# Moving memory rows, late tables and conditioning weights back, and crossing two groups by halves, in a two-block transformer kernel

## The reference, cut to what matters

```python
mod = silu(c) @ ada_w[layer] + ada_b[layer]          # 6 x 1024
sh1, sc1, g1, sh2, sc2, g2 = split(mod, 6)
h = rmsnorm(x, norm_g[layer, 0]) * (1 + sc1) + sh1
z, xbc, dt_raw, qkv = split(h @ ab_w_in, ...)        # product "in0"
y = concat([ssd_branch(z, conv5(xbc), dt_raw), neighbourhood_attention(qkv)])
x = x + g1 * rmsnorm(y @ ab_w_out)                   # product "out0"
h = rmsnorm(x, norm_g[layer, 2]) * (1 + sc2) + sh2   # needed by product "up0"
```

## Time and profile before

| | |
|---|---|
| median of three runs | 1597.03 us (1594.93 to 1597.8) |
| profiled execution: its own time, its span | 1598.08 us, 1596.3 us |
| mean granted clock of TensorE | 0.974 of full |
| busy: PE, DVE, ACT, POOL | 93%, 72%, 50%, 5% of the span |
| chain that ended last | PE 46%, DVE 21%, PE's weight loads 15%, issue 8%, ACT 7%, DMA 2% |
| chain from 0 to 120 us, largest lines | DMA of the stream 27.2%, DVE L2182 16.3%, DVE L1310 14.7%, DVE L1171 6.6% |

### The profile page before, as it was taken

How to read it: one execution, slowest core, us unless ns; L and a number is a source line. 1 busy time by engine, 2 the same in 40 slices (tenths; PEclk the granted TensorE clock), 3 DMA queues, 4 the chain that set the end, 5 groups by cost and what they waited for, 6 DMA issues and landing times.

```text
span 1596.3 us, 22352 instructions
## 1 busy us (share of the span) xinstructions
PE 1489.3 (93%) x8907; PEld 1276.0 (80%) x8910; DVE 1142.4 (72%) x1824; ACT 791.3 (50%) x1079; POOL 83.7 (5%) x82
## 2 busy tenths in 40 slices
PE   4779998999999999999999999889999899999998
PEld 3778875789988888877899888756786578799987
DVE  6797775599866857666786567999985675466653
ACT  4646654454533536454555435556554634354442
POOL 0000000000000000000000002940020000000000
PEclk7889999999999999999999999999999899999999
DMA  9864623369778553335566555333334243245551
GB/s 387 348 232 188 237 89 121 148 238 359 286 280 332 193 180 138 132 132 211 196 229 236 174 211 193 133 106 107 131 136 163 92 149 122 90 160 184 185 191 63
DMA packets 42518, 298.57 MB, mean 187 GB/s; under 512 B 4656, under 2 KB 4912, under 8 KB 7472
## 3 DMA queue, kind: packets, MB, share of 16 engines
q1 hardware_dynamic: 39984, 283.52, 47.9%
q0 software_dynamic: 1568, 8.39, 1.4%
q10 hardware_dynamic: 864, 5.24, 0.9%
HBM read 292.94 MB, written 4.19 MB: 186 GB/s over the span
## 4 chain that ended last, share of the span: by engine, by line
PE 46%; DVE 21%; PEld 15%; issue 8%; ACT 7%; DMA 2%; PEldq 1%; SPq 0%; ACTq 0%; DVEq 0%
PE ps L1034 19%; PE ps L1042 15%; PEld ps L1034 8%; PEld ps L1042 6%; DVE ring_at_lo L1310 6%; ACT w_hi L1299 3%; PE ps L1075 2%; DMA ring_at<-stream 2%; DVE ring_at L1171 2%; PE ps L2616 1%; DVE arena_at L2182 1%; DVE arena_at L3183 1%; PE ps L3527 1%; DVE arena_at L3192 1%; PE ps L3086 1%
## 5 line engine op out<-in xcount | busy, mean ns | idle before, releaser
L1310 DVE TENSOR_TENSOR ring_at_lo<-ring_at,w_hi 128x2048 fp32r<-128x2048 f32 (+1 forms) x218 | 496.3, 2279 | 179.4 <-ACT w_hi L1299 179.0
L1299 ACT ACTIVATE w_hi<-ring_at 128x2048 fp32r<-128x2048 f32 (+1 forms) x218 | 412.3, 1898 | 191.8 <-PE ps L1034 122.9
L1034 PE MATMUL ps<-w_hi,arena_at_lo 128*128 128x512 f32 x1104 | 305.1, 398 | 1.6 <-DVEq L4476 0.8
L1042 PE MATMUL ps<-h_hi,w_hi 128*128 128x256 f32 x1440 | 243.2, 292 | 14.8 <-DVE ring_at_lo L1310 7.8
L1034 PEld LDWEIGHTS ps<-w_hi,arena_at_lo 128*128 128x128 f32 x1104 | 204.6, 188 | 49.3 <-issue 2.7
L1042 PE MATMUL ps<-h_hi,ring_at_lo 128*128 128x256 f32 x1440 | 233.2, 284 | 0.0
L1042 PE MATMUL ps<-hT_at_lo,w_hi 128*128 128x256 f32 x1440 | 232.2, 284 | 0.0
L1042 PEld LDWEIGHTS ps<-h_hi,w_hi 128*128 128x128 f32 x1440 | 202.7, 193 | 23.0 <-issue 16.6
L1042 PEld LDWEIGHTS ps<-hT_at_lo,w_hi 128*128 128x128 f32 x1440 | 200.6, 192 | 0.0
L1042 PEld LDWEIGHTS ps<-h_hi,ring_at_lo 128*128 128x128 f32 x1440 | 199.1, 192 | 0.0
L1034 PE MATMUL ps<-ring_at_lo,arena_at_lo 128*128 128x512 f32 x552 | 172.1, 393 | 0.0
(11 more groups left out here) (464 smaller groups left out, 1662.9 us busy)
## 6 DMA issues: line engine op xcount, KB each, us to landing
ring_at<-stream SPq DMA_DIRECT2D x266, 1024.0 KB, 4.9
arena_at_lo<-kept_hi POOLq DMA_DIRECT2D x4, 1024.0 KB, 7.2
arena_at<-bias ACTq DMA_DIRECT2D x4, 768.0 KB, 8.0
kept<-arena_at POOLq DMA_DIRECT2D x4, 512.0 KB, 4.2
arena_at<-kept ACTq DMA_DIRECT2D x2, 1024.0 KB, 5.9
x_res<-x SPq DMA_DIRECT2D x1, 1024.0 KB, 10.5
arena_at<-mem POOLq DMA_DIRECT2D x1, 1024.0 KB, 12.7
kept_hi<-arena_at_lo POOLq DMA_DIRECT2D x1, 1024.0 KB, 10.5
```

The source lines that it names most:

```text
L1034: mm = pe.matmul(k.ps[:, bank + t, :], x_tile(f, slice(t * P, (t + 1) * P)), w, start=first and n == 0, stop=last and n == 2)
L1042: mm = pe.matmul(k.ps[:, bank + q // 2, (q % 2) * TOK:(q % 2 + 1) * TOK], w[:, q * P:(q + 1) * P], x, start=first and n == 0 and q % 2 == ...
L1299: act.activation(k.w_hi[:, s % HI, 0:n, :], k.ring[:, c % RING, 0:n, :], ACT.Identity).then_inc(k.hi_done, 1)
L1310: dve.tensor_tensor(k.w_lo[:, c % RING, 0:n, :], k.ring[:, c % RING, 0:n, :], k.w_hi[:, s % HI, 0:n, :].bitcast(F32), ALU.subtract).then_i ...
```

## The change

1. The first four own chunks of in0 are (0,0), (1,0), narrow, (0,1), then (1,1). Groups 2 and 3 stand behind the first and the second. The opening makes the high and low part of (1,0) behind half 0 of `h`, the low part in the midst of the dots of group 2. The norm's last transposes go to another PSUM bank.
2. Groups 4, 5, 6 stand behind own chunks 12, 16, 20 of in0 instead of 2, 5, 8; groups 7, 8, 9 behind chunks 3, 5, 7 of out0 instead of 11, 14, 17 of in0. Two waits of PE for guests are dropped.
3. The load of the memory rows waits until four own chunks are used, MemRates and MemTurn move from main steps 6 to 14 to 17 to 25, BiasLoad from 16 to 28, the late tables from behind stream chunk 10 to 13, and Inputs from step 6 to 10. SsdSteps is paced from 11 instead of 8, Ssd from 16 instead of 15.

```diff
-GUESTS = {"in0": [-1, -1, 0, 0, 2, 5, 8, 11, 14, 17], "up0": ...
+GUESTS = {"in0": [-1, -1, 0, 1, 12, 16, 20], "out0": [3, 5, 7], "up0": ...
+ORDER = {"in0": [(0, 0), (1, 0), (0, 1), (1, 1)] + [(g, j) for g in range(2, 11) for j in range(2)], ...
-        own.insert(1, ("narrow", NARROW[name], 0, None))
+        own.insert(2 if name == "in0" else 1, ("narrow", NARROW[name], 0, None))
...
     def gpsimd(self, pool, st):                     # MemTurn
         pool.wait_ge(*self.norm.m["bank_turned"].at(4))
+        pool.wait_ge(k.chunk_used, self.after)      # mem_turn.after = 4
         pool.dma_start(self.rows, k.mem_dram).then_inc(k.mem_in, 16)
...
-        return (4, 5, 6, 2)[f // 2]                 # FirstNorm.bank
+        return 4 + f // 2
...
-        split_hi(k, act, self.first_own + 2)        # FirstProduct.scalar, ahead of high(1)
+        split_hi(k, act, self.first_own + 3)
...
-        self.opening_dots(dve, 2)                   # FirstProduct.vector
+        self.opening_dots(dve, 2, (0, 1))
+        split_lo(k, dve, self.first_own + 2)
+        self.opening_dots(dve, 2, (2, 3))
         self.opening_dots(dve, 3)
         self.take_opening(dve, st, 2)
         self.take_opening(dve, st, 3)
-        split_lo(k, dve, self.first_own + 2)
+        split_lo(k, dve, self.first_own + 3)
         self.norm.low(dve, 1)
...
-        pe.wait_ge(k.guest_took, self.guests)       # SsdNorm and Mlstm
...
-    steps_due = paced([(0, 7, 8, 36)])
-    ssd_due = paced([(0, 7, 15, 22), (7, 13, 22, 29), ...
+    steps_due = paced([(0, 7, 11, 36)])
+    ssd_due = paced([(0, 7, 16, 22), (7, 13, 22, 29), ...
-        Woven(k, in0, (Threaded(Inputs(k)), paced([(0, 1, 6, 7)])),
-              (Threaded(mem_rates), paced([(0, 2, 6, 10)])), (Threaded(mem_turn), paced([(0, 4, 6, 14)])),
-              (Threaded(tables), paced([(0, 1, 16, 17)])),
+        Woven(k, in0, (Threaded(Inputs(k)), paced([(0, 1, 10, 11)])),
+              (Threaded(mem_rates), paced([(0, 2, 17, 19)])), (Threaded(mem_turn), paced([(0, 4, 17, 25)])),
+              (Threaded(tables), paced([(0, 1, 28, 29)])),
...
-                if c == 10:                         # SP: the late tables
+                if c == 13:
```

More of the change, by code:

```diff
@@ L98 @@
 MEM_AT = {"up0": 0, "in1": 1, "up1": 2, "in2": 3}
-GUESTS = {"in0": [-1, -1, 0, 0, 2, 5, 8, 11, 14, 17], "up0": [1, 3, 5, 7, 9, 11], "down0": [1, 4, 7, 10, 13],
+GUESTS = {"in0": [-1, -1, 0, 1, 12, 16, 20], "out0": [3, 5, 7],
+          "up0": [1, 3, 5, 7, 9, 11], "down0": [1, 4, 7, 10, 13],
           "out1": [3], "up1": [3, 9]}
@@ L124 @@
 HALVES = [(0, 0), (1, 0), (0, 1), (1, 1)]
-ORDER = {"xo": HALVES, "mix_out": HALVES, "xq": HALVES,
+ORDER = {"in0": [(0, 0), (1, 0), (0, 1), (1, 1)] + [(g, j) for g in range(2, 11) for j in range(2)], "xo": HALVES, "mix_out": HALVES, "xq": HALVES,
          "gate_up": HALVES + [(g, j) for g in range(2, FF2T // 2) for j in range(2)]}
@@ L1232, in follow @@
         self.norm, self.cond_in = norm, cond_in
-        self.opening = self.guests_after.pop(-1) + self.guests_after.pop(0)
+        self.opening = self.guests_after.pop(-1) + self.guests_after.pop(0) + self.guests_after.pop(1)
     def tensor(self, pe):
@@ L1249, in scalar, with opening_dots @@
         self.norm.high(act, st, 0)
-        split_hi(k, act, self.first_own + 2)
+        split_hi(k, act, self.first_own + 3)
         self.norm.high(act, st, 1)
         yield from super().scalar(act, st)
-    def opening_dots(self, dve, n):
-        for q in range(4):
+    def opening_dots(self, dve, n, qs=range(4)):
+        for q in qs:
             self.guest_dots(dve, n, self.opening[n][1], q)
@@ L2223, in __init__ @@
         super().__init__(k)
-        self.first, self.guests, self.z_in = in0.first_group, k.guests, z_in
+        self.first, self.z_in = in0.first_group, z_in
         self.xc, self.zs, self.zs_r, self.xc_r, self.rows = xc, zs, zs_r, xc_r, rows
@@ L2541, with __init__ @@
 class Mlstm(Stage):
-    def __init__(self, k, qT, kT, v, o, sel, gate, h, e, sc, small, junk, hi, lo, first, guests, o_in):
+    def __init__(self, k, qT, kT, v, o, sel, gate, h, e, sc, small, junk, hi, lo, first, o_in):
         super().__init__(k)
@@ L2547, in __init__ @@
         self.h, self.e, self.sc, self.small, self.junk = h, e, sc, small, junk
-        self.hi, self.lo, self.first, self.guests, self.o_in = hi, lo, first, guests, o_in
+        self.hi, self.lo, self.first, self.o_in = hi, lo, first, o_in
         self.steps = [("cell", i) for i in range(5)] + [("norm", 0), ("cell", 5), ("turn", 0), ("cell", 6), ("turn", 1),
@@ L2601, in out @@
             if i == 0:
-                pe.wait_ge(k.guest_took, self.guests)
                 pe.wait_ge(*self.gate.m["gates_in"].at(2))
@@ L2824, in layer1_stages @@
     gate.follow(in1)
-    cell = Mlstm(k, qT, kT, v, o, sel, gate, h, e, sc, sm, junk, hi, lo, first, k.guests, o_in)
+    cell = Mlstm(k, qT, kT, v, o, sel, gate, h, e, sc, sm, junk, hi, lo, first, o_in)
     cell.after = mem
@@ L4391, in all_stages @@
     tables = BiasLoad(k, table, bias, mem_turn, mem_rates)
+    mem_turn.after = 4
     in0 = in0_stage(k, xp, xc, zs, qT, kT, v, z_in, Conditions(k, mods), first_norm, mem_turn.stored)
@@ L4398, in all_stages @@
     src = Joined(Operand(None, norm.zs_r, norm.xc_r, norm.made), KD, Operand(None, na_hi, na_lo, na.made))
-    out0 = PostProduct(k, "out0", src, y, junk, small)
+    out0 = PostProduct(k, "out0", src, y, junk, small, Conditions(k, mods))
     out0.at_row = at_c
@@ L4403, in all_stages @@
     out0.follow(gain)
-    steps_due = paced([(0, 7, 8, 36)])
-    ssd_due = paced([(0, 7, 15, 22), (7, 13, 22, 29), (13, 19, 29, 36), (19, 21, 38, 40), (21, 54, 40, 76)])
+    steps_due = paced([(0, 7, 11, 36)])
+    ssd_due = paced([(0, 7, 16, 22), (7, 13, 22, 29), (13, 19, 29, 36), (19, 21, 38, 40), (21, 54, 40, 76)])
     norm_due, na_in, na_out = paced([(0, 4, 76, 84)]), paced([(0, 6, 81, 92)]), paced([(6, 19, 0, 24)], True)
```

## The result

The changed kernel takes 1598.55 us (median of 20 runs), the kernel before 1595.97 in runs on the same chip: a ratio of 1.0018, with a 95% interval of 1.0011 to 1.0026. By the ratio it is 2.9 us slower (the medians are 2.6 apart). That is less than the 3.2 us that I count as no difference, but the interval over 20 runs leaves out 1, so the sign is sure, and it is not the sign of my forecast (1594.7). The profiled execution has a span of 1600.4 us, 4.1 more than the one before; its own time, 1602.28, lies 3.7 above the median, so its losses are on the large side.

What follows compares the result with a forecast made beforehand. Arrivals were taken to bound the opening of in0 and DVE what follows; start -5.5, later in0 +1.5 and out0 +1.7 sum to -2.3 us, so a median of 1594.7 us, range 1589.5 to 1600.5.

Steps and rivals of the forecast that it cites:

- The opening: Start of in0: (1,0) fills PE's 5.8 us gap before the narrow chunk; (0,1) starts at 48.8 instead of 46.10.
- PE waits for [the late tables] inside the narrow chunk, which costs nothing, as (0,1) waits until 48.8 anyway: Narrow chunk of in0: tables end about 47.4, and PE's wait for them costs nothing.
- The memory rows: In (1,1) of in0: issued at 56.4, landing after 7.5 us (bounds 5.4 and 12.7); PE stands 4 to 5 us.
- my list: DVE's low splits in in0 of (2,1), (3,0) and two further, forecast at 73.7, 83.8, 95.8, 102.3.
- The mark: Second crossing of `x` to rows in in0: at 113.4 instead of 118.96; the start gives 5.5 us.
- The SSD norm: Later in in0: group 6's four dots land where DVE's norm chain is the path; costs 1.5 us, bounds 0 and 4.7.
- Rival B: Dots between out0's heads stop the attention: 5 us over forecast with five on the path, all twelve 1607; chance 0.12.
- A: Start of in0: memory rows there at 59.4 and Ln finds its table, giving 11.7 us in all, 1588.5; chance 0.25.
- C: Start of in0: memory rows as slow as now, 12.7 us; the start gives 0.3, time 1599.9; chance 0.13.
- out0's term: out0: twelve dots go in, nine fit into DVE's waits, last chunks come just in time; costs 1.7 us, bounds 0.5 and 5.
- I am wrong if ... out0 grows by more than 3: Sign against the forecast: out0's length, forecast up 1.7 us, growing by more than 3.

Runs made afterwards that it cites:

- no_cross: Changed kernel with the old order of own chunks (0,0), narrow, (0,1), (1,0) and the old opening; 1602.12 us, ratio 1.0042 to the kernel before.
- rows3: Changed kernel with the memory rows loaded once three own chunks are used instead of four; 1593.65 us, ratio 0.9989 to the kernel before.
- steps: Changed kernel with the second Ln of SsdSteps placed ahead of the first Silu; 1595.58 us, ratio 1.0006 to the kernel before.
- g_late: Changed kernel with groups 4 to 8 behind in0's chunks 10, 12, 14, 16, 18 and group 9 behind out0's chunk 1; 1591.8 us, ratio 0.9975.
- inp12: Changed kernel with the wait for the late tables one main step later; 1600.65 us, ratio 1.0034 to the kernel before.
- best1: Changed kernel with the edits of rows3, inp12 and steps, and groups 7 to 9 behind out0's chunks 1, 3, 5; 1587.52 us, ratio 0.9945.
- best2: Changed kernel with the edits of rows3, inp12 and steps, and the guest groups placed as in g_late; 1582.43 us, ratio 0.9918.
- short9: Changed kernel with group 9's dots over 16 columns instead of 1024, leaving out most of its sums; 1597.81 us, ratio 1.0014.

## Why the prediction was right and wrong

- **The opening: right, but for a gap.** (1,0) runs behind the first chunk, after 1.2 us of wait for its low part, where I had no gap. The crossing alone is worth the little that the bound by arrivals and DVE leaves (no_cross).
- **"PE waits for [the late tables] inside the narrow chunk, which costs nothing, as (0,1) waits until 48.8 anyway": wrong by 1.1.** The masks end the wait at 48.44 (I had 47.4), six matmuls follow, and (0,1) starts at 49.89.
- **The memory rows: right, mis-sized by 0.7.** 8.2 us instead of 7.5, inside my bounds, and issued 0.8 later, at 57.2, so PE stood 6.0 us and not 4 to 5; rows3 shows that their landing sets the start. Together with the tables this is the 1.3 to 1.7 us by which DVE's splits are behind my list. Their distances, made of 2.2, 1.6, 0.8 and the table load, hold.
- **The mark.** -3.7 instead of -5.5, but the first transposes behind it run at full clock where the earlier trace rows have them at 1.85 us for eight, now 1.06, so the heads are at -5.3. Two errors of mine met there, and luck: the five other kernels with this opening have their heads at -3.5 to -4.6.
- **The SSD norm: right in the mean.** 2.1 instead of 1.5 in this trace (-5.3 to -3.2); in the other kernels with group 6 behind chunk 20 it is 0.9 to 2.4, mostly 1.2, and in one (steps) nothing. Without that group there (g_late) the stretch costs nothing.
- **Rival B (dots between heads): refuted.** The one dot that I counted cost 1.2 (-3.1 to -1.9), as I had it, and the others nothing, or 1.5 more in no_cross, inp12 and steps; B had five dots on the path.
- **Rivals A and C.** C is out: the rows took 8.2 us and not 12.7. A said what the start would give, 11.7 us, with the rows there in time and Ln ahead of the table load; best1 and best2, which do both, have their heads 12.7 and 11.7 ahead. The changed kernel did neither.
- **The step that failed is out0's term: "its last own chunks and the memory chunks come just in time. This costs 1.7 us."** It measured 7.2 in the profiled execution, and 4.1 to 7.2 in the seven kernels with this placing: 1.2 by the dot at 293, 0.8 by group 9 at the end, 2.5 by the late load and 2.7 by the clock that PE loses in the wait. I had the 1.2 and 0.5 of the 0.8. The loads, said to come "just in time", and the clock stood at nothing, and they are 5.2. "I am wrong if ... out0 grows by more than 3" was the right alarm. A part of it could be had before: the place in the stream by counting seven slots back over the guests, and the time of that chunk's use from SP's issues, which before come at 299.9 and 306.7 for own chunks 4 and 5. On the clock of before, own chunk 5's use at 306.7 and 5.0 us of landing give 311.7, and ACT comes for the chunk at 310.85: 0.9 late. The 1.6 of the slow load I could not have read there, since before the POOL fetch stands 3.0 us ahead of SP's load and slows nothing (5.2).

The profiled execution of the changed kernel shows 4.1 us, the ratio 2.9; the tail differs between executions, and this one had the largest that I saw.

## What to carry to other kernels

- When loads wait for a slot of a ring, write the stream down in its new order and count back the ring's size from each chunk whose consumer comes early: moved weights cost not only the engine that reads them, but also push the load of all that stands behind them to a later release. It shows in the trace as several issues at once where there was one at a time. Look as well at what another queue issues just ahead of such a load.
- A stall on the way of PE is to be priced with the clock behind it: here 3.3 us of delay cost 6.0. Put work that is off PE's path where PE has no wait (five groups cost nothing there), not where the stage hands over to the next.
- Where a wait is bound by an arrival, moving it doesn't help; asking for the data earlier does (4.6 us for one number in the kernel).

## What the runs showed of the hardware that I had not expected

- What a wait costs in clock jumps with its length. PE's wait ahead of the memory product and the time of its 36 matmuls: 1.1 to 2.5 us of wait, 8.6 us (eight kernels); 2.65, 2.80 and 3.44, 10.2 (steps, no_cross, rows3); 3.42 and 4.40, 11.4 (short9, changed). The same opening with waits of 3.4 to 4.8 us had its full clock back from 52 us on in the changed kernel, and only between 53 and 55 in the five others.
- Loads of one queue were not slowed by those behind them, and were where another queue's stood just ahead: three 1 MB loads of SP issued within 0.9 us land after 4.7 to 5.1, 6.8 to 7.2 and 8.9 to 9.8 us, and the first alone after 4.7 to 5.2; with a 1 MB fetch by POOL 1.8 to 2.0 us ahead the first takes 5.7 to 6.7, with the fetch 3.0 us ahead 4.7 to 5.2.
- Fourteen filling matmuls kept the clock at 1.00 and saved 0.6 us of the tail, nothing that the ratio shows: they ended some 2 us after DVE's last low part was there.
